# First layer norm: scale and offset after the transposes on ScalarE, the stored tiles finished by GpSimd, the first two value tiles in passes

## The reference, cut to what matters

```python
def layer_norm(x, g, b):
    mu = jnp.mean(xf, axis=-1, keepdims=True)
    var = jnp.mean(jnp.square(xf - mu), axis=-1, keepdims=True)
    y = (xf - mu) * lax.rsqrt(var + LN_EPS)
    return (y * g.astype(jnp.float32) + b.astype(jnp.float32)).astype(x.dtype)
...
h = layer_norm(x, ln0_g, ln0_b)
proj = jnp.einsum('bsd,dn->bsn', h, w_in[i])
...
h = layer_norm(DEEPNORM_ALPHA * h + mix, ln1_g[i], ln1_b[i])
```

## Time and profile before

| | us |
|---|---|
| median of 3 runs | 1636.98 (1636.86 to 1637.41) |
| the profiled execution | 1637.65 |
| its span on the core | 1635.8 |
| first value matmul in it | 17.99 |
| block `f` begins in it | 71.16 |

### The profile page before, as it was taken

How to read it: one execution, slowest core, us unless ns; L and a number is a source line. 1 busy time by engine, 2 the same in 40 slices (tenths; PEclk the granted TensorE clock), 3 DMA queues, 4 the chain that set the end, 5 groups by cost and what they waited for, 6 DMA issues and landing times.

```text
span 1635.8 us, 21111 instructions
## 1 busy us (share of the span) xinstructions
PE 1588.1 (97%) x7800; PEld 1325.1 (81%) x7800; DVE 1150.4 (70%) x1724; ACT 744.0 (45%) x1162; POOL 694.2 (42%) x487
## 2 busy tenths in 40 slices
PE   6999999999999999999999989999999999999996
PEld 4888888888888887888887868888888888888886
DVE  8558878437767668656336879986666579857977
ACT  3245454327888774511233644445444553433342
POOL 5222221522333145564443597765566323223334
PEclk9999999999999999999999999999999999999999
DMA  8211110101010143521333435554444598867672
GB/s 295 77 42 38 27 39 27 39 29 38 27 53 27 39 117 97 147 78 52 122 120 118 164 126 183 182 195 143 159 168 152 185 330 254 272 199 238 194 204 104
DMA packets 220693, 208.51 MB, mean 127 GB/s; under 512 B 9000, under 2 KB 190504, under 8 KB 218544
## 3 DMA queue, kind: packets, MB, share of 16 engines
q1 hardware_dynamic: 217424, 196.09, 38.7%
q10 hardware_dynamic: 3168, 11.08, 1.7%
HBM read 160.96 MB, written 46.17 MB: 127 GB/s over the span
## 4 chain that ended last, share of the span: by engine, by line
PE 83%; DVE 5%; ACT 4%; DMA 2%; POOL 2%; issue 2%; SPq 0%; DVEq 0%; ACTq 0%; POOLq 0%
PE dense L969 7%; PE dense L971 7%; PE dense L973 7%; PE dense L979 4%; PE dense L1315 3%; PE dense L1317 3%; PE dense L1316 3%; PE dense L1395 3%; PE dense L1396 3%; PE dense L1397 3%; PE mixA L1106 2%; PE dense L1047 2%; PE dense L1049 2%; PE dense L1048 2%; PE mixA L1315 2%
## 5 line engine op out<-in xcount | busy, mean ns | idle before, releaser
L969 PE MATMUL dense<-parts 128*128 128x512 f32 x528 | 183.3, 409 | 1.6 <-DVE page L2090 0.9
L943 POOL TENSOR_TENSOR parts<-page,parts 128x512 fp32r<-128x512 f32 x52 | 88.9, 1733 | 208.1 <-ACT parts L1909 208.1
L862 POOL TENSOR_TENSOR parts<-page,parts 128x512 fp32r<-128x512 f32 x108 | 156.3, 1469 | 44.9 <-ACT parts L1788 41.6
L971 PE MATMUL dense<-parts 128*128 128x512 f32 x528 | 174.0, 391 | 0.0
L973 PE MATMUL dense<-parts 128*128 128x512 f32 x528 | 173.3, 390 | 0.0
L854 POOL CAST parts<-page 128x1024 fp32r<-128x1024 f32 x43 | 49.3, 1145 | 287.4 <-PE dense L973 192.4
L905 POOL TENSOR_TENSOR page<-page 128x512 f32<-128x512 f32 x80 | 122.6, 1532 | 59.8 <-PE dense L1317 25.2
L913 POOL TENSOR_TENSOR parts<-page,parts 128x512 fp32r<-128x512 f32 x80 | 114.8, 1437 | 55.4 <-ACT parts L1835 50.6
L1919 ACT CAST parts<-page 128x1024 fp32r<-128x1024 f32 x56 | 58.8, 1055 | 142.8 <-DVE page L2614 123.2
L973 PEld LDWEIGHTS dense<-parts 128*128 128x128 f32 x528 | 99.1, 188 | 21.8
L971 PEld LDWEIGHTS dense<-parts 128*128 128x128 f32 x528 | 99.1, 188 | 21.0
(11 more groups left out here) (298 smaller groups left out, 4315.8 us busy)
## 6 DMA issues: line engine op xcount, KB each, us to landing
page<-in_w_ff SPq DMA_DIRECT2D x104, 512.0 KB, 6.0
page<-in_w_in SPq DMA_DIRECT2D x120, 256.0 KB, 3.2
page<-act_scratch SPq DMA_DIRECT2D x56, 512.0 KB, 5.7
act_scratch<-page SPq DMA_DIRECT2D x16, 1024.0 KB, 3.9
act_scratch<-page SPq DMA_DIRECT2D x16, 768.0 KB, 7.0
page<-in_w_o SPq DMA_DIRECT2D x32, 256.0 KB, 3.1
h_scratch<-page ACTq DMA_DIRECT2D x8, 512.0 KB, 3.5
page<-c_scratch SPq DMA_DIRECT2D x8, 512.0 KB, 5.0
```

The lines of the kernel that those rows point to most:

```text
L862: ins = nc.gpsimd.tensor_tensor(R(lo, at, HALF), F(raw_page(c), at, HALF), R(hi, at, HALF).bitcast(F32), ALU.subtract)
L969: mm(o, whi, x_, start=first, stop=False)
L971: mm(o, whi, x_, start=False, stop=False)
```

## The change

VectorE makes only (x - mean) * rstd, in one pass (L2136 of the new code). g and b are loaded also as 16 rows of 128 and turned by TensorE into 16 columns, `gb`. ScalarE, after the transposes, applies them in place in PSUM with eight ACTIVATEs per tile (L1521: scale `gb[k]`, offset `gb[8 + k]`, each a value per partition), and then takes the high part. GpSimd finishes the token-by-token tile (`whole_token`: times g, plus b, in four 128x512 operations), for the six first tiles ahead of chunk 4 and for the two last ahead of chunk 6. ScalarE issues each store after `h_full`. The first two value tiles are computed in passes (`first_values`): all eight high x high matmuls, then low x high, then high x low, of both tiles mixed. The loads are dealt out anew.

```diff
-            sp.dma_start(F(PG_X), x_t[0]).then_inc(x_in[0], 16)
-            for c in range(C_END):
+            sp.dma_start(F(PG_X, 0, HALF), x_t[0][:, 0:HALF]).then_inc(x_in[0], 16)
+            sp.dma_start(F(PG_X + 1), x_t[1]).then_inc(x_in[1], 16)
+            for c in range(2, C_END):
+                if c == 3:
+                    continue
                 if c == C_AB:
                     for w in range(GN):
                         load_gate(w)
                 load_chunk(c)
-                if c == 3:
-                    for t in range(4, TT):
+                if c == 2:
+                    for t in range(2, TT):
                         sp.dma_start(F(PG_X + t), x_t[t]).then_inc(x_in[t], 16)
+                        if t == 2:
+                            sp.dma_start(F(PG_G0), row(ln0_g)).then_inc(g0_in, 16)
+                            sp.dma_start(F(PG_B0), row(ln0_b)).then_inc(b0_in, 16)
...
+            def whole_token(t):
+                tile = lambda at: F(PG_X + t, at, HALF)
+                pool.wait_ge(h_turned, t + 1)
+                for at in (0, HALF):
+                    ins = nc.gpsimd.tensor_tensor(tile(at), tile(at), F(PG_G0, at, HALF), ALU.mult)
+                ins.then_inc(h_scaled, 1)
+                pool.wait_ge(h_scaled, AFTER_W0_LOW + t + 1)
+                for at in (0, HALF):
+                    ins = nc.gpsimd.tensor_tensor(tile(at), tile(at), F(PG_B0, at, HALF), ALU.add)
+                ins.then_inc(h_full, 1)
+
+            pool.wait_ge(g0_in, 16)
+            pool.wait_ge(b0_in, 16)
             for c in range(4, C_END):
+                for t in {4: range(0, 6), 6: range(6, TT)}.get(c, ()):
+                    whole_token(t)
...
-                    if (name, t, k % 2) == ("vhg", 0, 0):
-                        pe.wait_ge(w0_split, k // 2 + 1)
...
+            gb_turned = dense[1][:, HALF:HALF + 2 * KD]
+            nc.tensor.transpose(gb_turned, F(PG_COLS, 0, P)[0:2 * KD, :], ident[0:2 * KD, 0:2 * KD])
...
+            def first_values(t, n, ks):
+
+                j = JOB["vhg", t]
+                out1 = dense[SET[j]][:, 0:HALF]
+                x_, base = (XHI, XLO, XHI)[n], (WHI, WHI, WLO)[n]
+                for k in ks:
+                    if t == 0 and n != 1 and k % 2 == 0:
+                        pe.wait_ge((w0_hi, None, w0_split)[n], k // 2 + 1)
+                    ins = mm(out1, R(x_ + k, t * P, P), R(base + k // 2, (k % 2) * HALF, HALF),
+                             start=n == 0 and k == 0, stop=n == 2 and k == KD - 1)
+                if n == 2 and ks[-1] == KD - 1:
+                    end(ins, j)
+
+            every, early, late = range(KD), range(KD - 2), range(KD - 2, KD)
             turn_tokens(0)
-            for t in range(TT):
+            turn_tokens(1)
+            begin(JOB["vhg", 0])
+            pe.wait_ge(h_hi, 1)
+            first_values(0, 0, every)
+            pe.wait_ge(h_split, 1)
+            first_values(0, 1, every)
+            first_values(0, 2, range(0, 2))
+            begin(JOB["vhg", 1])
+            pe.wait_ge(h_hi, 2)
+            first_values(1, 0, every)
+            first_values(0, 2, range(2, 4))
+            pe.wait_ge(h_split, 2)
+            first_values(1, 1, every)
+            turn_tokens(2)
+            first_values(0, 2, range(4, 6))
+            first_values(1, 2, early)
+            first_values(0, 2, late)
+            first_values(1, 2, late)
+            for t in range(2, TT):
...
-            act.dma_start(F(PG_G0), row(ln0_g)).then_inc(rows_in, 16)
-            act.dma_start(F(PG_B0), row(ln0_b)).then_inc(rows_in, 16)
+            act.dma_start(F(PG_X, HALF, HALF), x_t[0][:, HALF:]).then_inc(x0_in, 16)
             act.dma_start(ident[:, :], c_ident).then_inc(ident_in, 16)
-            for t in range(1, 4):
-                act.dma_start(F(PG_X + t), x_t[t]).then_inc(x_in[t], 16)
+            for i, vec in enumerate((ln0_g, ln0_b)):
+                act.dma_start(F(PG_COLS, 0, P)[i * KD:(i + 1) * KD, :], vec.rearrange("(k n) -> k n", k=KD)).then_inc(ident_in, 16)
+            for c in (0, 1, 3):
+                for i in range(2):
+                    act.dma_start(F(PG_W0 + c, i * HALF, HALF), w_views["in"][:, 2 * c + i, C_HI:C_HI + HALF],
+                                  ).then_inc(w0_landed[c], 16)
...
             def tokens_high(t):
+                mixed = (mixA, mixB)[t % 2]
                 act.wait_ge(h_turned, t + 1)
+                if t == 0:
+                    own_step(nc.scalar.copy(gb[:, :], dense[1][:, HALF:HALF + 2 * KD]))
+                for k in range(KD):
+                    cols = mixed[:, k * P:(k + 1) * P]
+                    ins = A(cols, cols, ACT.Identity, scale=gb[:, k:k + 1], bias=gb[:, KD + k:KD + k + 1])
+                own_step(ins)
                 nc.scalar.copy(x_hi_all[:, :, t * P:(t + 1) * P],
-                               (mixA, mixB)[t % 2][:, :].rearrange("q (k n) -> q k n", k=KD)).then_inc(h_hi, 1)
+                               mixed[:, :].rearrange("q (k n) -> q k n", k=KD)).then_inc(h_hi, 1)
+
+            def store_tokens(t):
+                act.wait_ge(h_full, t + 1)
                 act.dma_start(h_scratch[t], F(PG_X + t)).then_inc(h_stored[t % 2], 16)
-            rstd_estimate(0)
-            for j in range(4):
+            gb = lbt[:, :, :].rearrange("q a n -> q (a n)")
+
+            def weight_high_0(j):
                 act.wait_ge(w0_landed[j], 32)
                 nc.scalar.copy(R(WHI + j), F(PG_W0 + j)).then_inc(w0_hi, 1)
-                if j == 1:
-                    tokens_high(0)
-                    rstd_estimate(1)
-            for t in range(1, TT + 1):
+
+            rstd_estimate(0)
+            weight_high_0(0)
+            rstd_estimate(1)
+            tokens_high(0)
+            weight_high_0(1)
+            rstd_estimate(2)
+            weight_high_0(2)
+            tokens_high(1)
+            weight_high_0(3)
+            rstd_estimate(3)
+            tokens_high(2)
+            for t in range(2):
+                store_values(PG_VHG, "vhg", t, 0)
+            for t in range(3, TT + 1):
                 if t + 1 < TT:
                     rstd_estimate(t + 1)
                 if t < TT:
                     tokens_high(t)
                 store_values(PG_VHG, "vhg", t - 1, 0)
+                store_tokens(t - 3)
+            for t in range(TT - 2, TT):
+                store_tokens(t)
...
             def tokens_norm(t):
-                norm_apply(F(PG_X + t), F(PG_X + t), t % 2, F(PG_G0), F(PG_B0), t).then_inc(h_ready, 1)
+                i, tile = t % 2, F(PG_X + t)
+                dve.wait_ge(var_ready, t + 1)
+                then(half_var(i))
+                dve.wait_ge(rs_est, t + 1)
+                newton(i)
+                V.tensor_scalar(tile, tile, mv[:, i, 0:1], rstd[:, i, 2:3], ALU.subtract, ALU.mult).then_inc(h_ready, 1)
...
-            tokens_stats(1)
-            norm_begin(F(PG_X + 1), F(PG_X + 1), 1, F(PG_G0), 1)
-            tokens_low(0)
-            norm_end(F(PG_X + 1), 1, F(PG_B0), 1).then_inc(h_ready, 1)
-            for t in range(1, TT):
+            for t in range(TT):
+                tokens_norm(t)
                 if t + 1 < TT:
                     tokens_stats(t + 1)
-                    tokens_norm(t + 1)
-                tokens_low(t)
+                if t:
+                    tokens_low(t - 1)
+            tokens_low(TT - 1)```

How the order moves at the places that the prediction speaks of, each engine's instructions in its fixed order (`parts3` are the weights' parts, `parts11` and `parts19` the high and low parts of the turned tiles, `page27` the tiles, `dense0` and `dense1` the results of even and odd value tiles).

ScalarE, from the first tile's estimate to the fourth weight page, before:

```order
L1445 ACTIVATE rstd<-mv,eps 128x1 [waits var_ready,const_set]
L1446 ACTIVATE rstd<-rstd 128x1 [waits act_step]
L1464 CAST parts3<-page35 128x1024 [waits w0_landed0]
L1464 CAST parts3<-page43 128x1024 [waits w0_landed1]
L1457 CAST parts11<-mixA 128x8x128 [waits h_turned]
L1459 DMA h_scratch<-page27 128x1024
L1445 ACTIVATE rstd<-mv,eps 128x1 [waits var_ready]
L1446 ACTIVATE rstd<-rstd 128x1 [waits act_step]
L1464 CAST parts3<-page43 128x1024 [waits w0_landed2]
L1464 CAST parts3<-page43 128x1024 [waits w0_landed3]
```

More of the change, by code:

```diff
@@ L97 @@
 XHI, XLO = 11, 19
-PG_X, PG_G0, PG_B0 = 27, 38, 39
+PG_X, PG_G0, PG_B0, PG_COLS = 27, 38, 39, 36
 PG_HQ, PG_HB, PG_HK, PG_GATE = 27, 29, 31, (33, SPARE)
@@ L1998, in _, with norm_stats @@
             V.memset(eps[:, 1:2], RMS_EPS).then_inc(const_set, 1)
-            def norm_stats(src, i):
+            def norm_stats(src, i, second=None):
                 V.bn_stats(stats[:, i, 0, :], src[:, 0:HALF])
+                if second is not None:
+                    dve.wait_ge(*second)
                 then(V.bn_stats(stats[:, i, 1, :], src[:, HALF:]))
```

20 lines of the change are left out of this document (11 added, 9 removed).

## The result

| | before | after |
|---|---|---|
| device time, median of 4 runs | 1637.2 us (1636.86 to 1637.95) | **1659.78 us** (1655.07 to 1662.13) |
| profiled execution: time, span | 1637.65, 1635.8 | 1662.13, 1660.3 |
| tile 2 begins | 33.81 | 38.83 |
| a turn of the loop (tiles 2 to 7) | 6.34 | 10.05 |
| block `f` begins | 71.16 | 96.34 |

The ratio is 1.0138, 95% interval 1.0125 to 1.015: slower, by 22.6 us. The forecast was 1653.0, the range 1643 to 1660.

What follows compares the result with a forecast made beforehand. TensorE's unbroken work was taken to bound the kernel, so only the `f` block's start mattered: 4.7 us at the start plus 11.3 in the loop, 16.0, gave 1653.65, or 1653.0 as median; range 1643 to 1660.

Steps and rivals of the forecast that it cites:

- The mechanism and its size: ScalarE's eight ACTIVATEs lengthen the chain from turning a tile to multiplying it: +4.7 us at the start, +11.3 in the loop.
- the signs: Eight in 2.9 us, TensorE waits of 2.1 before tiles 2 to 7, transposes 8.6 apart, `f` at 87.
- The eight ACTIVATEs: ScalarE's scale and offset pass per turned tile: 2.95 us, bounds 1.45 and 3.7; called the main term.
- rival 1: The eight ACTIVATEs are as cheap as plain PSUM copies, 1.45 us, giving 1641; chance 0.07.
- The start: Before the loop: ScalarE's queue delays the fourth weight page to 22.7, tile 2 begins at 38.5 instead of 33.81, +4.7 us.
- the 30 matmuls: TensorE before turning tile 2: 13 at 0.427 and 17 at 0.228, 9.4 us.
- tile 2's chain: From turning tile 2 to its first matmul, over ScalarE and VectorE: 6.40 us, hiding 12 matmuls, ending at 38.5.
- The 0.7 put down for the wait on tile 2: ScalarE's queue at the start: tile 2's estimate stands ahead of weight 2 and that tile lands late, up to 0.7 us.
- The covers: GpSimd's tile completion, ScalarE's later stores, the new load order and VectorE's work stay hidden; all costed at nothing.
- rival 3: The loop's waits drop TensorE's clock: 2.7 us for each of six tiles, 1669; chance 0.05.
- The rival's price: Rival 3's cost per tile: nine matmuls and the transposes on the path at the slow clock, 2.7 us, six times.
- The passes over the first two tiles: At the start, first matmul about 14.5 instead of 17.99, a gain more than given back by tile 2.

Runs made afterwards that it cites:

- second profile of after: The changed kernel itself run once more, with nothing altered: 1659.1 us (1658.45 to 1662.67).
- the early turn: Changed kernel with tiles turned two jobs ahead, fourth weight page split before second token tile, tile 2 turned after tile 0's second pass: 1637.2 us, ratio 1.0002.

## Why the prediction was right, point by point

- **The mechanism and its size.** The chain alone was worth 4.7 + 11.3 = 16.0 us in the prediction. Measured with the clock taken out: 5.0 at the start and 5 x (8.49 - 6.34) = 10.75, together 15.8. The 5.0 is one execution's: tile 2 began at 38.27 in the second profile of after and at 39.70 without GpSimd's work.
- **Partly luck.** The loss was 22.6 us and the mechanism that was forecast gives 15.8 of it. The rest came from a mechanism held for unlikely, and the median still fell inside the range, by 0.2 us, because the range had been stretched to 1660 for dear ACTIVATEs, which did not come. Two of the four runs lie above it. Of the signs, ScalarE's eight came as said; the transposes were to be 8.6 us apart and are 10.05, and `f` was to begin at 87 and begins at 96.34.
- **The eight ACTIVATEs**, the main term: 2.95 predicted, 2.87 measured. The means lay near: 459 ns from the earlier trace rows, 441 measured. The choice of the row with both pointers, over the plain copy's 264, was what made the forecast; by the copy (rival 1) it would have been 1641, and even the eight without pointers come to 1643.9. By the distance of their starts, (2.87 - 0.44)/7 = 0.347, then 0.255 and 0.166 us, a pointer costs 0.09, and neighbours overlap by 0.09 to 0.12. (The Trainium skill, ScalarE: Activation LUTs, What ACT_TABLE_LOAD costs, gives 93 ns for a pointer and 93 of overlap, and the traces agree. Without pointers an estimate from its figures is 186 + 107 = 293 ns, measured 290; with two it is 479, measured 441, so that its 3.2 us for the eight came out too high.)
- **The start.** `h_ready` at 7.8 for 8.2, fourth weight page split at 22.8 for 22.7, the 30 matmuls 9.83 for 9.4, tile 2's chain 6.30 for 6.40, tile 2 at 38.83 for 38.5. One link was not foreseen: the first weight page landed at 10.23 and held ScalarE, so the eight began at 11.82, 1.4 late. The 0.7 put down for the wait on tile 2 didn't occur (it rested on the cast at 13.20 in the earlier trace rows, which is the second weight page's, not the third's; in after VectorE begins on tile 2 at 13.12 without waiting for it) and the other pieces were shorter, so the two errors cancelled. The pieces that the prediction lists add up to 22.85, not 22.7, which changes nothing. TensorE's wait for the page was 3.54, not 4 to 5. The 30 matmuls themselves vary: 8.45, 8.51, 8.69, 9.06, 9.36, 9.49, 9.52 and 9.83 us in the kernels that run them alike.
- **The covers.** GpSimd's operations took 1.28 and 1.31 us each, not 1.74, and 5.1 us a tile; it had chunks 4 and 5 done at 76.4, 20 us before `f` began, and for chunk 6 it waited itself (7.57 us idle before 96.64). ScalarE never idled on `h_full`. VectorE's wait for the last stores (12.9 us in all, before its masks) did not reach TensorE in after. Behind it masks and bounds took 11 us, from 101.96 to 113, where 6 were put down, and ScalarE waited for them until 112.17. All at nothing, as costed, and the kernel without GpSimd's work has the same time; but this last cover was thin, and once the early turn had taken the loss away TensorE waited there for 2.04 us.
- **The step that failed: rival 3, at 0.05.** "The waits of the loop drop TensorE's clock" happened, in most tiles. The forecast held it for unlikely by a wait of 1.11 us at the end of the kernel, after which the transposes were still fast. That row was true, and it was the right row for a wait of 1.1: the kernel with one pointer shows just that. It was read across to a wait of 1.85 to 2.1, nearly twice as long and in each turn, for which the row says nothing. What spoke for the rival, matmuls at 1.2 GHz after an idle time of 2.75 us, was nearer to the case. The term put at nothing: five waits and the last tile cost 9.4 us in the profiled execution (five times 10.06 - 8.49, and 1.5), less in others. The median lies 6.8 us above the central value, and the fastest run, 1655.07, 2.
- **The rival's price** was too high, 2.7 us a tile for 1.55 measured (at worst 9.4 in all, not 16). It took the nine matmuls and all of the transposes as slow; in after the clock was back at 2.4 GHz before the transposes or in them (1.04 to 1.49 us), and nine and transposes together lost 1.56 to 1.62 in each tile. Both are on the path; the fifteen matmuls behind them are not, since they run while the chain does. A turn of 8.48 and one of 10.05 stand side by side behind waits of 2.50 and 1.85. (The Trainium skill, TensorE: Matmul & The Clock Gate, What's actually happening, has it that activity releases the throttle, and that one kernel shows different numbers of slow matmuls at its start from run to run. The traces agree on the second: after's two profiles have slow matmuls behind tile 2's wait in one and none in the other.)
- **The passes over the first two tiles** started TensorE's matmuls at 15.8 instead of 17.99, and it was more than given back, as forecast. Even without the eight ACTIVATEs only 0.76 us of it is left at tile 2, and the kernel is level with before, not faster.

Open: whether GpSimd's activity has a small part in how often the clock falls, and what picks the tiles in which it does. No run separates that from chance. Open too, whether the last stores cost the early-turn kernels the 1.4 us that their start had gained: the part behind `f` takes 1562.4 to 1568.6 us over the profiles, 1568.6 in the one with the wait of 2.04.

## What to carry to other kernels

Moving a small pass onto an engine that is 45% busy costs time for every tile, when it enters a chain that the next tile's work waits for: its duration less the spare time of that chain (here 2.87 us against 0.87). Eight operations with two pointer operands cost twice what eight without do. Ask next what the wait does to TensorE: here 1.1 us was harmless, and 1.85 cost another 1.6 in most tiles; turning a tile one job earlier, with the order of the start mended, took away all of the loss. A row that shows that a short wait does no harm is evidence for waits of that length only. And when a loss has been taken away, look for the next wait: work that was costed at nothing was hidden behind the loss.

## What the runs showed of the hardware

- More work made the kernel faster: eight unused matmuls of 512 columns in each wait, 1.97 us, brought 8 us, as the granted clock of a turn rose from 0.83 to 1.00.
- The clock can fall after the work has begun again, and later from turn to turn. In after, the first two matmuls from 58.92 start 0.34 and 0.28 apart, those from 59.54 0.43; from 48.88 only the first distance is short, from 89.15 the first four are. In the timeline:

```profile
58.92 0.50 PE L1069 MATMUL dense<-parts 128*128 128x512 f32 x1 [1.83 <-DVE parts L2122]
59.26 0.48 PE L1070 MATMUL dense<-parts 128*128 128x512 f32 x1
59.54 0.63 PE L1071 MATMUL dense<-parts 128*128 128x512 f32 x1
```

- In the start the profile's granted clock and the matmuls disagree: it reads 1.00 from 20 to 24 us in before, where matmuls start 0.43 apart. In the loop of after both agree: 0.54 of full speed from 38.83 to 42.57, and matmuls 0.43 apart.
- VectorE's pass with two scalars over 1024 columns takes 0.81 us alone (0.811 to 0.815 in the loop without GpSimd's work), and up to 1.90 beside GpSimd's sums on an earlier tile (with the scale alone: 44.43, while GpSimd was at work from 43.26 to 45.8). In after the pass at 39.58 kept its 0.81 and it was GpSimd's sum beside it, from 39.80, that took 1.73 instead of 1.25: either side can be the one that waits. None of these lay on the path.
